# Routed experts in a pipeline of fixed length with a loop of single blocks behind it

## The chip, the cores and the metric

The kernel runs on one core of one Trainium2 chip. The metric is the device time of one execution in microseconds (us). Lines (L2820) are those of the kernel before; in the order listings of the changed kernel they are those of its own file, some 3 to 110 lines further down.

## The reference

Two layers of a decoder trunk on 1024 tokens of 1024 values, in float32. Each layer has a mixer (attention and gated delta rule in layer 0, retention in layer 1) and then a mixture of experts. The change touches only the experts:

```python
g_prob = jax.nn.softmax(xt @ w_group + b_group)            # 4 groups
g_top, g_idx = lax.top_k(g_prob, 1)
e_top, e_idx = lax.top_k(e_logits_of_that_group, 2)        # 8 experts in a group
weights = g_top * softmax(e_top)
expert_id = g_idx * 8 + e_idx                              # 32 experts
# for each of the 2048 (token, expert) pairs:
hid = silu(xs @ w_gate[e]) * (xs @ w_up[e])                # 1024 -> 512
y[token] += (hid @ w_down[e]) * weight                     # 512 -> 1024
```

## The kernel before

**Blocks.** The pairs of an expert are laid out in blocks of `CAP` = 96 rows: `LOW` = 64 low ones and `REST` = 32 more. Every expert has one block, even an empty one; pairs beyond 96 go to overflow blocks behind the 32. Three blocks make a unit, and the number of units is rounded up, so that for up to one overflow block 33 blocks run. `route` works out on the chip, for each place of a block, the tokens (`r.token`), the destinations (`r.dest`), the expert (`r.expert`), a flag that says whether it has more than 64 rows (`r.full`), and in `r.used` the number of units. Its arrays have `NBLK` = 54 columns.

**A block** is, on PE: the gate and up products of the low rows (`gate_up_low`, L2820; two column halves of PE at once), if the flag is set those of the rest rows (`gate_up_rest`, L2830), the transposes of the hidden rows (`hid_turn`, L2840 and L2844), and the down products (`down_low`, L2852, and by the flag `down_rest`, L2860). ACT takes the silu (L2932, L2935), DVE multiplies (L2965), copies the turned hidden rows (L2971) and multiplies with the gate vector (L2977). `turn` (L2813) transposes the gathered token rows for the next block; ACT and DVE bring them to `xT`.

**The pipeline.** `experts` writes the program of each engine by hand. On PE a block b is: gates of b, `hid_turn` of b-1, `turn` for b+1, downs of b-1. So the chain from gates over silu and product to the transposes of one block lies beside the products of its neighbours. Three blocks of unit 0 are written out; then a loop runs over the units, three blocks in its body, as long as `r.used` says. At the head of each unit PE loads the flags of the last block and of its own three (`is_full`, L2889) into registers, and then issues the first low product. Behind the loop stand the `hid_turn` and downs of the last block.

**Weights.** A block's weights are 4 MB for gate and up and 2 MB for down. There are three slots for them (`u` = 0, 1, 2), and the block at place u of a unit takes slot u. The first three loads are issued in `route`'s stage. Then SP goes through a unit in the order gate-up 0, gate-up 1, down 0, gate-up 2, down 1, down 2. A gate-up load waits for the gates of the block that had the slot before, a down load for its downs, and each waits with all that is behind it in the queue.

**Rows.** On POOL the gather of the token rows for the block three places on (L2773) and the scatter of a finished block's rows (L2791) alternate: `gather(m, u)`, `scatter(m - 1, u)`. Each has a small copy of its indices ahead of it.

## Time and profile before

| | us |
|---|---|
| median of 3 runs (lowest, highest) | 3241.58 (3240.41, 3242.32) |
| the profiled execution | 3243.15 |
| its span, first to last instruction | 3241.4 |
| PE busy over the span | 2990.3 (92%) |
| DVE, ACT, POOL busy | 1322.1, 834.3, 701.4 |
| layer 0 experts: first low product to last down product | 965.0 to 1510.1 |
| layer 1 experts: the same | 2613.5 to 3163.6 |
| mean DMA rate over the span | 198 GB/s |

The two expert stages are 1095 us of the span. The page gives averages over all stages: PE is at 92% over all, and the DMA engines at 50 to 60%, while in the expert stages both are close to full. A stage must be read by its own stretches.

### The profile page before, as it was taken

How to read it: one execution, taken by the hardware profiler on the slowest of the kernel's cores; microseconds unless marked ns; L12 is line 12 of the kernel's file. 1: busy time of each engine (PE TensorE's matmuls, PEld its weight loads, DVE VectorE, ACT ScalarE, POOL GpSimd, SP SyncE). 2: the span in 40 equal slices, each digit the busy share in tenths (PEclk: the TensorE clock that was granted, in tenths of full speed). 3: DMA queues.
4: the chain of work that ended last, by engine and by line, in shares of the span. 5: the costliest groups of instructions: out<-in, count | busy, mean ns of one | idle time of the engine just before them, and what ended most of it. 6: DMA issues, size and time to landing. Idle time of an engine off the chain costs nothing. (4 is left out here: it accounts for less than half of the span.)

```text
span 3241.4 us, 45940 instructions
## 1 busy us (share of the span) xinstructions
PE 2990.3 (92%) x16555; PEld 1592.0 (49%) x16556; DVE 1322.1 (41%) x3214; ACT 834.3 (26%) x1707; POOL 701.4 (22%) x1075
## 2 busy tenths in 40 slices
PE   8989999598999999899899999999999989988786
PEld 6446544486444434333466666666444434333333
DVE  4377787573441222122644444444222311222124
ACT  2134343142121111010344445454301111111111
POOL 0000100471111122121633333332100011221213
PEclk9989999799999999999999999999999999999898
DMA  7300055233258999995611011110431297999975
GB/s 298 133 14 1 28 188 176 65 77 107 71 241 350 407 419 412 413 417 231 219 48 38 27 50 51 52 51 14 150 129 44 99 385 309 420 423 407 422 318 224
DMA packets 192256, 642.49 MB, mean 198 GB/s; under 512 B 54964, under 2 KB 114115, under 8 KB 157031
## 3 DMA queue, kind: packets, MB, share of 16 engines
q1 hardware_dynamic: 161670, 589.54, 46.9%
q0 software_dynamic: 20576, 42.01, 3.4%
q10 hardware_dynamic: 9856, 8.92, 0.8%
q8 instruction: 94, 1.54, 0.2%
q14 instruction: 60, 0.48, 0.1%
HBM read 614.61 MB, written 53.79 MB: 206 GB/s over the span
## 5 line engine op out<-in xcount | busy, mean ns | idle before, releaser
L2820 PE MATMUL f1e_pgu<-f1w_gu,f1e_xT 128*64 128x512 f32 x1056 | 251.2, 631 | 66.7 <-DMA f1w_gu<-in_moe_w_up_dram 54.8
L2820 PE MATMUL f0e_pgu<-f0w_gu,f0e_xT 128*64 128x512 f32 x1056 | 245.0, 618 | 30.0 <-issue 14.2
L1926 PE MATMUL mo_py<-mo_w,mo_tiles 128*128 128x512 f32 x512 | 220.9, 592 | 0.0
L2820 PEld LDWEIGHTS f1e_pgu<-f1w_gu,f1e_xT 128*64 128x64 f32 x1056 | 82.4, 145 | 227.6 <-issue 170.7
L2120 PE MATMUL ret_pa<-ret_w,hT_mix 128*128 128x384 f32 x512 | 175.8, 486 | 2.7 <-PEq L3007 2.7
L2820 PEld LDWEIGHTS f0e_pgu<-f0w_gu,f0e_xT 128*64 128x64 f32 x1056 | 80.8, 142 | 183.7 <-issue 169.1
L512 PE MATMUL gc_pq<-hT_mix,gc_w 128*128 128x512 f32 x384 | 169.3, 600 | 0.7 <-PEq L917 0.7
L2971 DVE COPY f1e_hidT<-f1e_ph 128x384 f32<-128x384 f32 x33 | 18.4, 557 | 338.1 <-PE f1e_ph L2844 338.1
L1926 PEld LDWEIGHTS mo_py<-mo_w,mo_tiles 128*128 128x128 f32 x512 | 96.8, 190 | 119.6 <-issue 119.6
L2971 DVE COPY f0e_hidT<-f0e_ph 128x384 f32<-128x384 f32 x33 | 18.4, 557 | 328.3 <-PE f0e_ph L2844 328.3
L2108 POOL TENSOR_TENSOR ret_z<-ret_z,ret_gain 128x256 f32<-128x256 f32 x64 | 46.4, 726 | 454.5 <-DVE ret_z L2409 454.5
L2852 PE MATMUL f1e_pd<-f1w_d,f1e_hidT 128*64 128x512 f32 x528 | 120.6, 598 | 1.0 <-DVE f1e_hidT L2971 1.0
L2852 PE MATMUL f0e_pd<-f0w_d,f0e_hidT 128*64 128x512 f32 x528 | 120.6, 598 | 0.9 <-DVE f0e_hidT L2971 0.9
L2120 PEld LDWEIGHTS ret_pa<-ret_w,hT_mix 128*128 128x128 f32 x512 | 92.6, 190 | 54.9 <-issue 3.0
L2932 ACT ACTIVATE f1e_hs<-f1e_pgu 128x256 f32<-128x256 f32 x33 | 12.6, 383 | 410.1 <-PE f1e_pgu L2820 410.1
L1818 POOL TENSOR_TENSOR mo_z<-mo_z,mo_bias_b 128x1024 f32<-128x1024 f32 x16 | 37.5, 2346 | 370.1 <-DVE mo_z L1795 370.1
L512 PEld LDWEIGHTS gc_pq<-hT_mix,gc_w 128*128 128x128 f32 x384 | 73.1, 192 | 90.4 <-issue 90.4
L1769 DVE TENSOR_TENSOR mo_z<-mo_py,mo_gate_b 128x1024 f32<-128x1024 f32 x16 | 19.6, 1224 | 237.7 <-PE mo_py L1926 237.7
L1926 PE MATMUL mo_py<-mo_w,mixT 128*128 128x512 f32 x256 | 112.8, 600 | 2.5 <-DMA mo_w<-in_hy_w_out_dram 2.5
L2932 ACT ACTIVATE f0e_hs<-f0e_pgu 128x256 f32<-128x256 f32 x33 | 12.6, 383 | 378.3 <-PE f0e_pgu L2820 378.3
L2120 PE MATMUL ret_pb<-ret_wsum,ret_hsum 128*128 128x384 f32 x256 | 91.3, 502 | 2.9 <-issue 2.9
L2787 POOL COPY f1e_didx<-f_dest 128x2 int32 x33 | 5.9, 179 | 380.1 <-DVE f1e_y L2977 304.7
(646 smaller groups left out, 5650.1 us busy)
## 6 DMA issues: line engine op xcount, KB each, us to landing
f0w_gu<-in_moe_w_gate_dram SPq DMA_DIRECT2D x33, 2048.0 KB, 18.6
f0w_gu<-in_moe_w_up_dram SPq DMA_DIRECT2D x33, 2048.0 KB, 26.9
f0w_d<-in_moe_w_down_dram SPq DMA_DIRECT2D x66, 1024.0 KB, 19.7
f1w_gu<-in_moe_w_gate_dram SPq DMA_DIRECT2D x33, 2048.0 KB, 20.0
f1w_gu<-in_moe_w_up_dram SPq DMA_DIRECT2D x33, 2048.0 KB, 31.2
f1w_d<-in_moe_w_down_dram SPq DMA_DIRECT2D x66, 1024.0 KB, 22.3
gc_land<-in_ada_w_dram SPq DMA_DIRECT2D x48, 512.0 KB, 4.9
mixT<-in_ada_w_dram SPq DMA_DIRECT2D x32, 512.0 KB, 4.7
```

What stands on the lines that cost most here:

```text
L512: mm = pe.matmul(pq[u][:, half * 512:(half + 1) * 512], w[u][:, kk, :], g.hT[:, kk, half * 512:(half + 1) * 512], start=(kk == 0), stop=(k ...
L1769: dve.tensor_tensor(z[:, :], y, self.gate_b[:, :], ALU.mult).then_inc(S["zmul"], 1)
L1818: pool.tensor_tensor(z[:, :], z[:, :], self.bias_b[:, :], ALU.add).then_inc(S["done"], 1)
L1926: mm = pe.matmul(py[t % 3][:, half * 512:(half + 1) * 512], rows_of(kk, t), ws[:, kk, half * 512:(half + 1) * 512], start=(kk == 0), stop= ...
L2108: pool.tensor_tensor(zb, zb, gain[:, h, :], ALU.mult).then_inc(S["gained"], 1)
L2120: mm = pe.matmul(bank[:, 0:HW], tokens[:, kk, :], weights[:, kk, :], start=(kk == 0 and not add), stop=(kk == KH - 1), skip_group_check=True)
L2787: pool.tensor_copy(didx[u][:, :], dst).then_inc(slots["didxd"][u], 1)
L2820: mm = pe.matmul(pgu[0][h * LOW:(h + 1) * LOW, :], xT[u][:, kk, 0:LOW], ew.gu[u][:, :, kk, h * FH:(h + 1) * FH], start=(kk == 0), stop=(kk ...
L2852: mm = pe.matmul(pd[0][h * LOW:(h + 1) * LOW, :], hidT_low[:, k % 2, k // 2, :], ew.d[u][:, k, h * DH:(h + 1) * DH], start=(k == 0), stop= ...
L2932: act.activation(hs[0][:, :], pgu[0][:, 0:FH], ACT.Silu).then_inc(S["silu_a"], 1)
L2971: dve.tensor_copy(hidT[:, :], ph[:, 0:4 * CAP]).then_inc(S["hTd"], 1)
```

## The change

Places. `SPARE` = 2 empty places stand ahead of the blocks: block 0 is now at place 2, slot 2 of unit 0, and block 31 at place 33, slot 0 of unit 11. `route` fills the tables two columns further on; they have 57 columns.

The pipeline runs the first `STEADY` = 31 blocks, always: four of them written out (unit 0's last and unit 1), then a loop from unit 2 to unit 10, whose bounds are constants. Behind it stand the `hid_turn` and downs of block 30, and then a loop of single blocks, from place 33 to the last one in use. It has at least one turn (block 31), and one more for each overflow block. All its blocks use slot 0. A weight load in it waits until the block before in slot 0 has done its gates (`gu_free`, counted by ACT) or its downs (`d_free`, by DVE). On PE a turn of the tail's loop is: low gates, rest gates, `hid_turn`, `turn` for the next place, downs; nothing of another block lies between.

The flags are loaded behind the low gate and up product of each block, and not at the head of the unit.

Cut to its core, the diff is:

```diff
+SPARE = 2
+STEADY = NE - 1
+NBLK = SPARE + PAIRS // CAP + NE
+NBLK = -(-NBLK // UNIT) * UNIT
...
     def first_loads(self, sp):
-        for u in range(UNIT):
-            self.load_gu(sp, u, u)
-            self.load_d(sp, u, u)
+        for n in range(UNIT):
+            self.load_gu(sp, (n + SPARE) % UNIT, n)
+            self.load_d(sp, (n + SPARE) % UNIT, n)
...
         @block.sync
-            with sp.Fori(1, units_used(sp)) as m:
+            for m, u in STARTING[UNIT:]:
+                gate_up_weights(m, u, nth(m, u) - 1)
+                down_weights(m, u, nth(m, u) - 1)
+            with sp.Fori(FIRST_UNITS, LAST_UNIT + 1) as m:
                 now = [sp.value_load(expert[0:1, bass.ds(m, 1), u], min_val=0, max_val=NE - 1) for u in range(UNIT)]
                 for u in range(UNIT + 1):
...
+            with sp.Fori(TAIL, places_end(sp)) as p:
+                e = sp.value_load(r.expert[0:1, bass.ds(p, 1)], min_val=0, max_val=NE - 1)
+                sp.wait_ge(S["gu_free"], tail_held(p) - 1)
+                ew.load_gu(sp, 0, e)
+                sp.wait_ge(S["d_free"], tail_held(p) - 1)
+                ew.load_d(sp, 0, e)
...
         @block.gpsimd
-            with pool.Fori(1, units_used(pool)) as m:
+            for m in range(1, 3):
+                for u in range(UNIT):
+                    if m * UNIT + u >= SPARE + UNIT:
+                        gather(m, u)
+                        scatter(m - 1, u)
+            with pool.Fori(3, LAST_UNIT + 1) as m:
                 for u in range(UNIT):
...
+            with pool.Fori(TAIL, places_end(pool)) as p:
+                tail_gather(p + 1)
+                tail_scatter(p)
...
         @block.tensor
+            def block_of(m, u, prior=None, first=False):
+                mb, ub = preceding(m, u)
+                low_gates(u, held(m, u), nth(m, u))
+                if prior is None and not first:
+                    prior = is_full(mb, ub)
+                second = is_full(m, u)
+                rest_gates(u, second)
+                if not first:
+                    hid_turn(nth(mb, ub))
+                turn(*following(m, u))
+                if not first:
+                    downs(ub, held(mb, ub), nth(mb, ub), prior)
+                return second
...
-            with pe.Fori(1, units_used(pe)) as m:
-                prior = is_full(m - 1, UNIT - 1)
-                second = [is_full(m, u) for u in range(UNIT)]
-                for u in range(UNIT):
-                    gates(m, u, second[u])
...
+            with pe.Fori(FIRST_UNITS, LAST_UNIT + 1) as m:
                 for u in range(UNIT):
+                    prior = block_of(m, u, prior if u else None)
+            prior = is_full(*END)
+            hid_turn(nth(*END))
+            downs(END[1], held(*END), nth(*END), prior)
+            with pe.Fori(TAIL, places_end(pe)) as p:
+                low_gates(0, tail_held(p), tail_nth(p))
+                second = pe.value_load(r.full[0:1, bass.ds(p, 1)], min_val=0, max_val=1)
+                rest_gates(0, second)
+                hid_turn(tail_nth(p))
+                turn_rows(0, tail_held(p + 1), tail_nth(p + 1))
+                downs(0, tail_held(p), tail_nth(p), second)
```

ACT and DVE get the same division: four blocks, the loop, the tail's loop. On DVE a turn of the tail is product, copy of the turned rows, `take`, gate multiplication.

**PE, head of the loop over units, layer 0.** The flags (`f_full`) before:

```order
L2902 ISA
L2889 TENSOR_LOAD f_full
L2889 ISA x3
L2889 TENSOR_LOAD f_full
L2889 ISA x3
L2889 TENSOR_LOAD f_full
L2889 ISA x3
L2889 TENSOR_LOAD f_full
L2889 ISA x2
L2877 ISA
L2820 MATMUL f0e_pgu<-f0w_gu,f0e_xT 64x512 x16
```

and now:

```order
L2995 ISA
L2962 ISA
L2754 REGISTER_ALU
L2901 MATMUL f0e_pgu<-f0w_gu,f0e_xT 64x512 x16
L2958 ISA
L2958 TENSOR_LOAD f_full
L2958 ISA x3
L2958 TENSOR_LOAD f_full
L2958 ISA x2
L2969 COMPARE_AND_BRANCH
L2911 MATMUL f0e_pgu<-f0w_gu,f0e_xT 32x256 x32
```

The four loads ahead of the low product (L2820, now L2901) are two behind it, and the other two stand behind the low products of the unit's second and third block.

**PE, the end of layer 0's experts.** The `hid_turn` and downs of the last block before:

```order
L2738 TENSOR_LOAD f_used
L2738 ISA x2
L2836 ISA
L2743 REGISTER_ALU
L2840 MATMUL f0e_ph<-ident,f0e_hid 128x128 x2
L2844 MATMUL f0e_ph<-ident,f0e_hid 64x64 x4
L2889 ISA
L2889 TENSOR_LOAD f_full
L2889 ISA x2
L2866 ISA
L2852 MATMUL f0e_pd<-f0w_d,f0e_hidT 64x512 x8
```

and now, from the downs of block 30 into the tail's loop:

```order
L2933 MATMUL f0e_pd<-f0w_d,f0e_hidT 64x512 x8
L2952 COMPARE_AND_BRANCH
L2941 MATMUL f0e_pd<-f0w_d,f0e_hidT 32x256 x16
L2952 UNCONDITIONAL_BRANCH
L2954 UNCONDITIONAL_BRANCH
L2746 TENSOR_LOAD f_used
L2746 ISA x2
L3001 UNCONDITIONAL_BRANCH
L3001 ISA
L2962 REGISTER_ALU
L2754 REGISTER_ALU
L2901 MATMUL f0e_pgu<-f0w_gu,f0e_xT 64x512 x16
```

Before, the program ends with this block's downs. Now the downs of block 30 stand there with no low product beside them, and the first low product of the tail comes behind the load of the count (`f_used`).

**SP, the first loads of layer 0's expert stage** (the numbers behind `gu` and `d` are the slots). Before, from the first load of the first turn of the loop:

```order
L2689 DMA f0w_gu0<-in_moe_w_gate_dram 128x4096
L2690 DMA f0w_gu0<-in_moe_w_up_dram 128x4096
L2754 REGISTER_ALU
L2689 ISA
L2689 DMA f0w_gu1<-in_moe_w_gate_dram 128x4096
L2690 DMA f0w_gu1<-in_moe_w_up_dram 128x4096
L2694 DMA f0w_d0<-in_moe_w_down_dram 128x2048
L2694 ISA
L2694 DMA f0w_d0<-in_moe_w_down_dram 128x2048
L2689 ISA
L2689 DMA f0w_gu2<-in_moe_w_gate_dram 128x4096
```

and now, from the start of the stage:

```order
L2695 DMA f0w_gu2<-in_moe_w_gate_dram 128x4096
L2696 DMA f0w_gu2<-in_moe_w_up_dram 128x4096
L2700 DMA f0w_d2<-in_moe_w_down_dram 128x2048 x2
L2796 UNCONDITIONAL_BRANCH
L2796 ISA
L2797 TENSOR_LOAD f0_expert
L2797 ISA x3
L2797 TENSOR_LOAD f0_expert
L2797 ISA x3
L2797 TENSOR_LOAD f0_expert
L2797 ISA x2
L2784 REGISTER_ALU
```

The down load of the fourth block (slot 2) now stands ahead of the fifth block's gate-up load; before, it came after it.

## Rows read from the trace of the kernel before

**Rows 1.** Both expert stages: us, five engines busy (x), PEclk, DMA share, GB/s
```profile
972.00:1455.00 483.00, 454.46 (x3366) 193.08 (x3366) 100.02 (x267) 60.03 (x180) 96.90 (x142) 0.98 0.97 403
2624.00:3118.00 494.00, 428.73 (x2824) 177.68 (x2822) 99.44 (x267) 59.16 (x179) 99.23 (x145) 0.94 0.95 393
```

**Rows 2.** PE waits, layer 0 (f0e), layer 1 (f1e): total us, times, longest
```profile
PE f0e_pgu L2820 <- issue: 14.2, 7, 2.9
PE f0e_pgu L2820 <- DMA f0w_gu<-in_moe_w_up_dram: 12.4, 3, 6.5
PE f1e_pgu L2820 <- DMA f1w_gu<-in_moe_w_up_dram: 54.8, 9, 10.7
```

**Rows 3.** Instructions of the gate-up product tile, layer 0: ns min/median/max
```profile
L2830 PE MATMUL f0e_pgu<-f0w_gu,f0e_xT x1088: 378/379/404, 982.2 to 1482.6; 128*32 128x256 f32 x182
```

**Rows 4.** Timeline of PE, layer 0, a block with rests: start us, us
```profile
1011.98 7.09 PE L2820 MATMUL f0e_pgu<-f0w_gu,f0e_xT 128*64 128x512 f32 x32 [2.92 <-issue]
...
1024.47 3.65 PE L2852 MATMUL f0e_pd<-f0w_d,f0e_hidT 128*64 128x512 f32 x16
1028.05 1.93 PE L2860 MATMUL f0e_pd<-f0w_d,f0e_hidT 128*32 128x256 f32 x32
1029.92 7.09 PE L2820 MATMUL f0e_pgu<-f0w_gu,f0e_xT 128*64 128x512 f32 x32
```

**Rows 5.** Timeline of PE: entry into the stage, and the head of a unit
```profile
951.49 11.27 PE L106 MATMUL f0e_pgu<-cos,ident 128*128 128x512 f32 x20 [2.71 <-PEq L2464]
...
1164.66 8.76 PE L2820 MATMUL f0e_pgu<-f0w_gu,f0e_xT 128*64 128x512 f32 x32 [2.50 <-issue]
```

**Rows 6.** PE sequencer, 1160 to 1166 and 1486 to 1500; then its timeline
```profile
L2889 PEldq TENSOR_LOAD <-f_full x4: 287/290/293, 1161.4 to 1163.7; - x4
L2902 PEldq COMPARE_BRANCH  x1: 215/215/215, 1161.0 to 1161.0; - x1
L2883 PEldq COMPARE_BRANCH  x1: 210/210/210, 1492.9 to 1492.9; - x1
1490.26 7.09 PE L2820 MATMUL f0e_pgu<-f0w_gu,f0e_xT 128*64 128x512 f32 x32
```

**Rows 7.** A ten-us stretch of layer 0, columns as in rows 1
```profile
1020.00:1030.00 10.00, 10.00 (x120) 5.00 (x113) 3.01 (x8) 1.67 (x5) 0.00 (x0) 1.00 0.19 77
```

**Rows 8.** PE timeline: gate-up weights of block 30, both layers
```profile
1454.71 8.78 PE L2820 MATMUL f0e_pgu<-f0w_gu,f0e_xT 128*64 128x512 f32 x32 [2.58 <-DMA f0w_gu<-in_moe_w_up_dram]
...
3117.84 10.08 PE L2820 MATMUL f1e_pgu<-f1w_gu,f1e_xT 128*64 128x512 f32 x32 [10.45 <-DMA f1w_gu<-in_moe_w_up_dram]
```

**Rows 9.** Timeline of SP's queue: weight loads issued
```profile
972.31 0.36 SPq L2689 DMA_DIRECT2D f0w_gu<-in_moe_w_gate_dram  x1
...
2624.47 0.35 SPq L2689 DMA_DIRECT2D f1w_gu<-in_moe_w_gate_dram  x1
...
2663.31 23.52 SPq L2694 DMA_DIRECT2D f1w_d<-in_moe_w_down_dram  x4
```

**Rows 10.** Timeline of PE: down products of the last block, both layers
```profile
1506.48 3.65 PE L2852 MATMUL f0e_pd<-f0w_d,f0e_hidT 128*64 128x512 f32 x16 [0.95 <-DVE f0e_hidT L2971]
...
3159.92 3.65 PE L2852 MATMUL f1e_pd<-f1w_d,f1e_hidT 128*64 128x512 f32 x16 [1.05 <-DVE f1e_hidT L2971]
```

**Rows 11.** POOL timeline, layer 0; gather landings from 1478 to 1480, and all
```profile
1473.91 0.18 POOL L2787 COPY f0e_didx<-f_dest 128x2 int32 x1 [15.60 <-DVE f0e_y L2977]
...
1478.30 1.06 POOL L2773 DMA_INDIRECT f_xg<-x,f0e_idx  x1 [0.88 <-POOL f0e_idx L2770]
...
1491.13 0.18 POOL L2787 COPY f0e_didx<-f_dest 128x2 int32 x1 [11.77 <-DVE f0e_y L2977]
...
DMA to landing us min/median/max: 7.0/7.0/7.0
DMA to landing us min/median/max: 7.0/11.7/16.9
```

**Rows 12.** DMA issues from 2624 to 2626: KB each, us to landing
```profile
f1w_gu<-in_moe_w_up_dram SPq DMA_DIRECT2D x1, 2048.0 KB, 13.1
```

More of the change, by code:

```diff
@@ L2743, in reach, with nth, held, tail_nth @@
                 eng.wait_ge(sem, value)
+        def nth(m, u):
+            return m * UNIT + u - (SPARE - 1)
+        def held(m, u):
+            return m + 1 if u >= SPARE else m
+        def tail_nth(p):
+            return p - (SPARE - 1)
+        def tail_held(p):
+            return p - (TAIL - LAST_UNIT - 1)
+        def following(m, u):
+            return (m, u + 1) if u < UNIT - 1 else (m + 1, 0)
+        def preceding(m, u):
+            return (m, u - 1) if u else (m - 1, UNIT - 1)
         expert = r.expert[:, :].rearrange("a (m u) -> a m u", u=UNIT)
@@ L2806, in turn, with turn_rows @@
             def turn(m, u):
-                pe.wait_ge(slots["x_in"][u], m * 16 + 16)
+                turn_rows(u, held(m, u), nth(m, u))
+            def turn_rows(u, landed, n):
+                pe.wait_ge(slots["x_in"][u], landed * 16)
                 for half in range(2):
-                    reach(pe, S["xd" if half else "xa"], m * UNIT + u)
+                    reach(pe, S["xd" if half else "xa"], n - 1)
                     for j in range(4):
@@ L2891, in _ @@
             g.keep_warm(pe, pgu[0][:, :], 10)
-            turn(0, 0)
+            turn(*STARTING[0])
             pe.wait_ge(S["cleared"], 2)
-            second = [is_full(0, u) for u in range(UNIT)]
-            for u in range(UNIT):
-                gates(0, u, second[u])
-                if u:
-                    hid_turn(0, u - 1)
-                turn(*((0, u + 1) if u < UNIT - 1 else (1, 0)))
-                if u:
-                    downs(0, u - 1, second[u - 1])
-            with pe.Fori(1, units_used(pe)) as m:
-                prior = is_full(m - 1, UNIT - 1)
-                second = [is_full(m, u) for u in range(UNIT)]
-                for u in range(UNIT):
-                    gates(m, u, second[u])
-                    hid_turn(*((m, u - 1) if u else (m - 1, UNIT - 1)))
-                    turn(*((m, u + 1) if u < UNIT - 1 else (m + 1, 0)))
-                    if u:
-                        downs(m, u - 1, second[u - 1])
-                    else:
-                        downs(m - 1, UNIT - 1, prior)
@@ L2913, in _ @@
-            end = unit_last(pe)
-            hid_turn(end, UNIT - 1)
-            downs(end, UNIT - 1, is_full(end, UNIT - 1))
+            prior = None
+            for m, u in STARTING:
+                prior = block_of(m, u, prior, (m, u) == STARTING[0])
+            with pe.Fori(FIRST_UNITS, LAST_UNIT + 1) as m:
+                for u in range(UNIT):
+                    prior = block_of(m, u, prior if u else None)
+            prior = is_full(*END)
+            hid_turn(nth(*END))
+            downs(END[1], held(*END), nth(*END), prior)
@@ L2977, in gate_rows, with block_of @@
                     dve.tensor_tensor(y[u][s][:, :], pd[s][:, 0:width], (r.gate if s == 0 else r.gate4)[:, :], ALU.mult)\
                         .then_inc(S[done], 1)
+            def block_of(m, u, first=False):
+                mb, ub = preceding(m, u)
+                n = nth(*following(m, u))
+                if not first:
+                    hid_copy(nth(mb, ub))
+                take(following(m, u)[1], n, n - UNIT)
+                hidden(nth(m, u))
+                if not first:
+                    gate_rows(ub, held(mb, ub), nth(mb, ub))
@@ L2997, in _ @@
-            end = unit_last(dve)
-            hid_copy(end, UNIT - 1)
-            gate_rows(end, UNIT - 1)
+            take(STARTING[0][1], 1, 0)
+            for n, (m, u) in enumerate(STARTING):
+                block_of(m, u, n == 0)
+            with dve.Fori(FIRST_UNITS, LAST_UNIT + 1) as m:
+                for u in range(UNIT):
+                    block_of(m, u)
+            hid_copy(nth(*END))
+            gate_rows(END[1], held(*END), nth(*END))
+            with dve.Fori(TAIL, places_end(dve)) as p:
+                hidden(tail_nth(p))
+                hid_copy(tail_nth(p))
+                take(0, tail_nth(p + 1), tail_nth(p))
+                gate_rows(0, tail_held(p), tail_nth(p))
```

232 lines of the change are left out of this document (127 added, 105 removed).

## The prediction

> **What bounds the kernel now.** The change touches the two expert stages only. So I read, in this order, the table of stretches over both stages, the waits of PE, the PE timeline block by block, the sequencer's own instructions, and the issues and landings of the weights.
>
> The stretches [rows 1] run from the first weight load inside a stage to the last gate-up arrival that PE waited for. PE is busy 454 of 483 us in layer 0 and 429 of 494 in layer 1. The DMA share is 0.97 and 0.95 there, so both resources are nearly full, and the stage goes at the pace of the weights with a little emptiness. PE's waits [rows 2] divide it: layer 0 has 12.4 us for gate-up weights and 14.2 us of "issue"; layer 1 has 54.8 us for weights.
>
> A block with over 64 rows also runs the "rest" products. The rest rows are 64 to a block: 1088/64 = 17 such blocks in layer 0 [rows 3]. Routing the given inputs by the reference gives the same 17, and 10 in layer 1. It also gives the largest expert: 88 pairs in layer 0 (no overflow, so the 33rd block of before is empty) and 100 in layer 1 (one overflow block of 4 rows). In layer 1 the first eight experts are full ones. A block costs PE 7.0 (low) + 1.9 (turns) + 3.6 (down low) = 12.5 us, with 3.6 + 1.9 more for the rests: 17.9 us from one low product to the next after the head of a unit [rows 4].
>
> At the head of a unit PE stands still 2.50 us after a block with rests, and the next low product takes 8.76 instead of 7.09 us, because the granted clock falls to its lower level for a while after the idle time [rows 5, 4]. The sequencer shows why: four flag loads, the first from 1161.4 and the last from 1163.7, some 0.77 us each with their register work, behind a loop branch of 0.215 us [rows 6].
>
> **What the change does, part by part.**
>
> 1. *Flags.* In each block one or two loads now stand behind the low product. The sequencer is ahead there: its branch behind the low product runs at 1492.9, and that product ends at 1490.26 + 7.09 = 1497.35 [rows 6]. Two loads (1.55 us) fit into 4.4 us of lead, so I cost them at nothing. The cover is the queued low product; without it they would cost 0.77 us each. The head of a unit then needs only the branch and register work: 1164.66 less 4 x 0.77 = 1161.6, before the old products end at 1162.16. So PE gains 2.5 + 1.7 = 4.2 us at a head that waits for nothing else. Whether the stage gains it is decided by the weights.
>
> 2. *Weights.* From the first load in the stage (972.3) to the gate-up arrival of block 30 (1454.7) are 482.4 us [rows 8, 9], in which 27 2/3 blocks are moved. I sum what the 49 and 50 ten-us stretches lack to a share of 1.00: 17.7 us in layer 0 (the largest is 8.1, at 1020 [rows 7]) and 29.5 in layer 1. That leaves 16.8 us a block in both: (482.4 - 17.7)/27.67 and (493.4 - 29.5)/27.67. The empty stretches arise where SP waits with the down load of a unit's last slot for a product in the next unit, and the next gate-up load is queued behind it (one such chain of 23.5 us at 2663 [rows 9]). The changed kernel has the same order in SP, one block later. The fourth block's down load now stands ahead of slot 0's, so the queue is empty some 7 us early in layer 0 (984 to 991) and 10 us in layer 1 (2635 to 2645). After that I follow the releases with PE blocks of 12.5 to 17.9 us and no gap at the heads: layer 0 empties for some 1 us more, layer 1 twice for 3.5 (before blocks 6 and 9) and, as before, 4 us later. That makes 8 in place of 17.7, and 21 in place of 29.5: the weights come 9.7 and 8.5 us earlier. The bounds are 0 (the heads' gain is lost in the new order) and 17.7 and 29.5 (no emptiness at all, which the first load chain excludes in part).
>
> 3. *End of layer 0.* 32 blocks, not 33. Gate-up of block 31 arrives at 972.3 + 28.67 x 16.8 + 8 = 1462. Block 28, in slot 0, starts three blocks earlier, at 1411.6. Then PE runs 28, 29, 30 (17.8 with a slow start, 14.4, 16.1) and the drain of 30 without cover: turns 0.9, a copy wait of 0.95 [rows 10], downs 5.5. That ends at 1467.3, later than the weights, so PE decides here. The tail block: 0.5 + 10.7 (gates) + 1.0 (silu and product, nothing beside it) + 0.9 + 1.1 (turns) + 5.5 (downs) = 19.7, so 1487.1 with 0.1 for the loop branch. Before: 1506.48 + 3.65 = 1510.1 [rows 10]. Gain 23.0 us.
>
> 4. *The gather in the tail.* PE's turn for the next place stands ahead of the downs. Its gather is queued in POOL behind the scatter of block 30. As in the loop now, that is 0.9 us from PE's end (1490.3) to the scatter's copy and 4.4 us from such a copy to the gather [rows 11]; I add 1 us for the tail's count, and a landing of 7.0 us in a nearly empty queue: 13.3 us after 1467.3. PE is there after 13.1. I cost it at 0.2 us, inside the rounding; it has no slack, and a landing of 11.7 (median) or 16.9 (longest) would be seen nearly in full.
>
> 5. *End of layer 1.* Still 33 blocks, the last two in the tail. Gate-up of block 31 arrives at 2624.5 + 28.67 x 16.8 + 21, about 3126.5. Gates with a slow clock 8.8: 3135.3. Only then may the load for the overflow block start, since the tail uses one slot: 1.1 us to the up issue, 13.1 us to its landing [rows 12]: 3149.5. Meanwhile PE does the turns and downs of block 31 and stands still for some 7 us. Then 8.8 + 1.35 + 0.97 + 1.1 + 3.65 = 15.9: 3165.4. Before: 3159.92 + 3.65 = 3163.6 [rows 10]. Loss 1.8 us: 8.5 gained on the way, and 10.3 paid for a load that is no longer beside other work.
>
> 6. *The rest.* Routing works on 57 columns instead of 54 and POOL clears two more tiles long before they are needed: 0.1 us. The last scatter of layer 0 now carries real rows: 0.3 us.
>
> The sum: -23.0 + 1.8 + 0.4 = -20.8 us. The profiled execution took 3243.15 us (its span 3241.4), so it would be 3222.3; the median of the runs is 3241.58, 1.6 us lower, and from there **3220.8 us**.
>
> The DMA page of the Trainium skill ("DMA: Bandwidth & Descriptors", Anatomy of one DMA) gives a fit of 2.0 us plus bytes over 436 GB/s. For the 4.19 MB of a gate-up pair that estimate is 11.6 us, 1.9 less than the 13.5 of the row. By it the forecast would be 3218.9. The row is of this kernel with gathers beside it, so it stands.
>
> **The rivals.**
>
> *The emptiness stays* (0.12). SP is still blocked by the last slot's down load, and one block later it may wait for as long. Then both arrivals come 9.7 and 8.5 us later: 3220.8 + 18.2 = 3239.0. For it: the order of the loads in SP is the same. Against: the largest holes follow the heads that now vanish.
>
> *The emptiness goes further* (0.08): another 6 us in each layer, 3209.
>
> *The flags are not covered* (0.05). If a load waited until the products before it were done, 40 of them in a layer at 0.77 us would be 31 us of PE, as much as is saved at the heads. What stays is the missing block, about -8: 3233. Against: at 1161.4 the first load ran while PE was still busy until 1162.16.
>
> *The jumps stall* (0.04). PE's entry into the stage shows 2.71 us of waiting for its sequencer [rows 5]; at five new jumps to a loop's head, its end and the tail that is 13.5 us on the path: 3234. For the loop branch itself the row says 0.215 us. The Trainium skill ("Runtime: NRT & Kernel Launch", Instruction fetch mechanics) says that a taken branch out of the fetched window waits for its target to be fetched; no row shows such a wait at a loop.
>
> *Slower: the tail's gathers are late* (0.08). Three gathers stand in the tails, each behind a scatter and ahead of downs. At 16.9 us instead of 7.0 they cost 9.7 in layer 0, and in layer 1 8.4 and 12, less 3 that the load hides: +27, so 3248. From a landing of about 14.7 us on, the kernel is slower than before. For it: the median is 11.7. Against: most run beside queued weights; this late one took 7.0.
>
> **How the numbers follow.** The forecast has the rest, 0.63. A measurement can tell 0.2%, 6.5 us, from no change. Faster by more than that: the forecast, the further gain, two fifths of the first rival and most of the two small ones, 0.82. Same: 0.10. Slower: 0.08. The range goes from 3204 (beyond the further gain, for sizes of 5 us in each end) to 3238, just short of the first rival's middle; outside lie the slower case, half of the first and a little below: 0.17.
>
> **What would show it.** The heads of units without "issue" waits and with low products of 7.09 us where no weights are late; SP's first two loads 20 us apart; 32 gate-up loads in layer 0; in layer 0 some 25 us from the arrival of block 31's gate-up weights to the last down product; in layer 1 one wait for weights of some 7 us in the last block. It is wrong if the flag loads leave holes between low and rest products, if the tail's turn waits for its gather, or if the ten-us stretches lack as much as before.

## The result and the profile after

The median of the changed kernel is 3220.73 us (4 runs, 3218.24 to 3223.56), beside 3241.2 us for the kernel before (4 runs, 3240.41 to 3242.32). The ratio is 0.9932, 95% interval 0.9919 to 0.9945. The forecast was 3220.8. The profiled execution took 3220.9 us; its span is 3218.6, 22.8 less than before.

A total that fits can hide terms that don't. So I cut both spans at three rows of TensorE: the first low product of a layer's experts, the first product of the combine behind them (f0c, f1c), and the same again in layer 1.

| stretch, us | before | changed | difference | forecast |
|---|---|---|---|---|
| start to layer 0's first low product | 965.0 | 965.9 | +0.9 | +0.1 |
| layer 0's experts, to the combine | 551.3 | 532.4 | -18.9 | -23.0 + 0.3 |
| combine to layer 1's first low product | 1097.2 | 1092.5 | -4.7 | 0 |
| layer 1's experts, to the combine | 556.3 | 556.2 | -0.1 | +1.8 |

The last stretch, from the combine to the end, is 71.6 us in both. Layer 0 gave less than forecast, and a stretch that the change doesn't touch gave 4.7 us. The experiments go after both.

TensorE's waits in the changed kernel (total us, times, longest us), beside [rows 2]:

```profile
PE f0e_pgu L2901 <- DMA f0w_gu<-in_moe_w_up_dram: 26.0, 6, 11.3
PE f1e_pgu L2901 <- DMA f1w_gu<-in_moe_w_up_dram: 59.7, 9, 11.1
```

The 14.2 us of "issue" of layer 0 are gone, and so are the 8.5 us that layer 1 had at four heads. The waits for weights rose from 12.4 to 26.0 us and from 54.8 to 59.7. In layer 0 nearly all that TensorE had stood idle at the heads it now stands idle at the loads, since it meets the weights sooner.

The table of stretches, beside [rows 1] (TensorE's busy time first, the granted clock and the DMA share near the end). Layer 1's line starts at 2618, 16 us behind the stage's first load (2601.62):

```profile
972.00:1462.00 490.00, 462.08 (x3479) 195.66 (x3476) 100.36 (x268) 60.73 (x182) 97.88 (x143) 0.98 0.97 405
2618.00:3105.00 487.00, 431.46 (x2794) 176.17 (x2792) 101.04 (x270) 57.51 (x175) 102.43 (x150) 0.94 0.96 397
```

In ten-us stretches, layer 0 lacks 15.9 us to a full DMA share from 970 to 1450 (17.7 before; forecast 8). Layer 1 lacks 27.7 us from 2600 to 3100, three us before the gates of block 31 (29.5 before; forecast 21). The hole that was 8.1 us deep at 1020 [rows 7] is gone, but there are others, early and late (the last line is layer 1's deepest early one):

```profile
980.00:990.00 10.00, 10.00 (x106) 5.15 (x104) 1.94 (x6) 2.06 (x6) 0.00 (x0) 1.00 0.68 290
990.00:1000.00 10.00, 10.00 (x64) 3.41 (x62) 1.39 (x4) 0.38 (x1) 3.47 (x5) 1.00 0.69 256
1330.00:1340.00 10.00, 10.00 (x72) 3.58 (x70) 2.67 (x8) 0.72 (x3) 2.36 (x4) 1.00 0.75 299
1430.00:1440.00 10.00, 10.00 (x63) 4.24 (x57) 3.33 (x9) 1.67 (x5) 1.59 (x3) 1.00 0.71 282
2610.00:2620.00 10.00, 10.00 (x104) 4.97 (x102) 2.32 (x7) 2.06 (x6) 0.00 (x0) 1.00 0.34 144
```

The end of layer 0 on TensorE's timeline (start us, us, and the idle time before it), beside [rows 8, 10]. It runs from the last products of block 30 through the tail's one block:

```profile
1467.85 3.65 PE L2933 MATMUL f0e_pd<-f0w_d,f0e_hidT 128*64 128x512 f32 x16 [0.88 <-DVE f0e_hidT L3071]
1471.44 1.93 PE L2941 MATMUL f0e_pd<-f0w_d,f0e_hidT 128*32 128x256 f32 x32
1473.55 7.09 PE L2901 MATMUL f0e_pgu<-f0w_gu,f0e_xT 128*64 128x512 f32 x32 [0.18 <-issue]
1480.57 3.66 PE L2911 MATMUL f0e_pgu<-f0w_gu,f0e_xT 128*32 128x256 f32 x64
1485.08 0.48 PE L2921 MATMUL f0e_ph<-ident,f0e_hid 128*128 128x128 f32 x2 [0.86 <-issue]
...
1490.52 1.93 PE L2941 MATMUL f0e_pd<-f0w_d,f0e_hidT 128*32 128x256 f32 x32
```

And the end of layer 1, from the gates of block 31 through the overflow block:

```profile
3103.12 8.78 PE L2901 MATMUL f1e_pgu<-f1w_gu,f1e_xT 128*64 128x512 f32 x32 [3.25 <-DMA f1w_gu<-in_moe_w_up_dram]
...
3125.33 8.56 PE L2901 MATMUL f1e_pgu<-f1w_gu,f1e_xT 128*64 128x512 f32 x32 [5.02 <-DMA f1w_gu<-in_moe_w_up_dram]
3135.23 0.48 PE L2921 MATMUL f1e_ph<-ident,f1e_hid 128*128 128x128 f32 x2 [1.34 <-DVE f1e_hid L3065]
```

### The profile page after: what moved, and what is told of

Its sections match the earlier page's. It is cut to its first block and busy times, and to the rows that moved or that the text cites. A ratio compares the mean times of both kernels' runs of the same rounds, so it can differ in the third digit from the quotient of the medians.

```text
span 3218.6 us, 45601 instructions
## 1 busy us (share of the span) xinstructions
PE 2973.8 (92%) x16489; PEld 1583.7 (49%) x16490; DVE 1317.4 (41%) x3205; ACT 832.2 (26%) x1701; POOL 698.2 (22%) x1074
## 5 line engine op out<-in xcount | busy, mean ns | idle before, releaser
L2901 PE MATMUL f1e_pgu<-f1w_gu,f1e_xT 128*64 128x512 f32 x1056 | 250.7, 630 | 63.0 <-DMA f1w_gu<-in_moe_w_up_dram 59.7
L2901 PE MATMUL f0e_pgu<-f0w_gu,f0e_xT 128*64 128x512 f32 x1024 | 231.5, 605 | 29.5 <-DMA f0w_gu<-in_moe_w_up_dram 26.0
L2901 PEld LDWEIGHTS f1e_pgu<-f1w_gu,f1e_xT 128*64 128x64 f32 x1056 | 81.7, 145 | 223.9 <-issue 221.9
L2901 PEld LDWEIGHTS f0e_pgu<-f0w_gu,f0e_xT 128*64 128x64 f32 x1024 | 75.8, 140 | 174.8 <-issue 173.5
L3071 DVE COPY f1e_hidT<-f1e_ph 128x384 f32<-128x384 f32 x33 | 18.4, 557 | 308.0 <-PE f1e_ph L2925 308.0
L2111 POOL TENSOR_TENSOR ret_z<-ret_z,ret_gain 128x256 f32<-128x256 f32 x64 | 46.4, 725 | 449.9 <-DVE ret_z L2412 449.9
L3024 ACT ACTIVATE f1e_hs<-f1e_pgu 128x256 f32<-128x256 f32 x33 | 12.6, 383 | 413.6 <-PE f1e_pgu L2901 413.6
L2123 PE MATMUL ret_pc<-ret_wsum,ret_hsum 128*128 128x384 f32 x256 | 87.9, 486 | 0.0
## 6 DMA issues: line engine op xcount, KB each, us to landing
f1w_gu<-in_moe_w_gate_dram SPq DMA_DIRECT2D x33, 2048.0 KB, 19.9
```

The costliest lines, as they stand in the source:

```text
L2111: pool.tensor_tensor(zb, zb, gain[:, h, :], ALU.mult).then_inc(S["gained"], 1)
L2123: mm = pe.matmul(bank[:, 0:HW], tokens[:, kk, :], weights[:, kk, :], start=(kk == 0 and not add), stop=(kk == KH - 1), skip_group_check=True)
L2901: mm = pe.matmul(pgu[0][h * LOW:(h + 1) * LOW, :], xT[u][:, kk, 0:LOW], ew.gu[u][:, :, kk, h * FH:(h + 1) * FH], start=(kk == 0), stop=(kk ...
L3024: act.activation(hs[0][:, :], pgu[0][:, 0:FH], ACT.Silu).then_inc(S["silu_a"], 1)
L3071: dve.tensor_copy(hidT[:, :], ph[:, 0:4 * CAP]).then_inc(S["hTd"], 1)
```

## The experiments

Twelve kernels ran. The times are medians, or a single time where the table shows no ratio. The stretches are cut as above, from each kernel's profiled execution.

| run | what | us | ratio to before (95%) | layer 0 | between | layer 1 |
|---|---|---|---|---|---|---|
| before | | 3241.2 | 1 | 551.3 | 1097.2 | 556.3 |
| changed | | 3220.7 | 0.9932 (0.9919 to 0.9945) | 532.4 | 1092.5 | 556.2 |
| e1 | only the flags | 3230.6 | 0.9960 (0.9945 to 0.9974) | 548.0 | 1096.9 | 546.7 |
| e2 | all but the flags | 3236.1 | 0.9985 (0.9970 to 0.9999) | 539.3 | 1092.5 | 566.2 |
| e3 | changed, SP's order | 3203.9 | 0.9881 (0.9864 to 0.9897) | 525.3 | 1092.5 | 548.5 |
| e4 | changed, no overflow block | 3197.7 | 0.9858 (0.9841 to 0.9874) | 532.3 | 1092.6 | 532.3 |
| e6 | changed, no overflow weights | 3213.6 | 0.9901 (0.9884 to 0.9919) | 534.6 | 1090.8 | 550.7 |
| e7 | e3 with another end | 3202.6 | 0.9869 (0.9852 to 0.9887) | 523.6 | 1097.3 | 544.8 |
| e5 | before, 172 dead matmuls | 3243.7 | 0.9999 (0.9989 to 1.0009) | 553.4 | 1091.7 | 556.2 |
| e5b | before, 40 dead matmuls | 3243.6 | 0.9999 (0.9989 to 1.0008) | 554.0 | 1091.6 | 556.1 |
| r1 | before again | 3244.8 | | 554.0 | 1092.2 | 557.0 |
| r2 | changed again | 3220.1 | | 532.3 | 1092.4 | 556.3 |
| e8 | changed, 4 loads of a flag | 3222.3 | | 532.7 | 1091.7 | 556.3 |
| e9 | changed, 8 loads of a flag | 3267.4 | | 561.3 | 1091.5 | 572.8 |

On the chips of the experiments the kernel before had medians of 3243.9, 3243.8, 3244.5 and 3246.4 us; the ratios are to those.

### e1 and e2: the change in two halves

e1 is the kernel before with this edit, and the same for the second place where the flags were read:

```diff
-                second = [is_full(m, u) for u in range(UNIT)]
+                prior = None
                 for u in range(UNIT):
-                    gates(m, u, second[u])
+                    prior, second = gates(m, u, prior)
```

where gates() now reads the flag behind gate_up_low(u).

> The kernel before with only the flags moved: each flag is loaded behind the low product of its block, in the old loop of units, with the 33rd (empty) block of layer 0 and the old end of layer 1. Theory (the flags free the heads of the units, and the weights decide what that is worth): no 'issue' waits at the heads; from the first low product to the combine layer 0 takes some 6 us less than 551.3, layer 1 some 9 us less than 556.3; the kernel 3226, between 3220 and 3232. Rival A (a load behind the low product holds up PE after all, 0.77 us each): 3236 to 3242, with holes between low and rest products. Rival B (the flags bring nothing alone, the fixed pipeline is the gain): 3238 to 3242, with no such holes.

e2 is the changed kernel with the flags at the head again (shown for the loop; the blocks written out ahead of it are changed likewise):

```diff
             with pe.Fori(FIRST_UNITS, LAST_UNIT + 1) as m:
+                prior = is_full(*preceding(m, 0))
+                flags = [is_full(m, u) for u in range(UNIT)]
                 for u in range(UNIT):
-                    prior = block_of(m, u, prior if u else None)
+                    prior = block_of(m, u, prior, False, flags[u])
```

> The changed kernel with the flags of a unit loaded at its head again; fixed pipeline and tail stay. Theory: the heads stand still 2.5 us again; layer 0 keeps only the block that falls away and the shorter end, 8 to 14 us less than before (551.3 from first low product to combine), and layer 1 pays for the load that nothing covers, 5 to 10 us more than before (556.3): the kernel 3232 to 3241. Rival (the fixed pipeline is the gain, the flags are not): 3221 to 3225.

Both theories held. Flags alone: layer 1 lost 9.6 us (forecast 9), layer 0 only 3.3 (forecast 6). The fixed pipeline alone: layer 0 lost 12.0 us, layer 1 gained 9.9. The two halves nearly add up: -15.4 and +0.3 us beside the changed kernel's -18.9 and -0.1. (Layer 0 of the kernel before takes up to 2.7 us more in other executions, see r1 below; against r1's 554.0, e1's gain there is 6.0, as expected.) So in layer 1 the change has two effects of nearly 10 us with opposite signs, and its zero is no sign that nothing happened. e2's last block shows the load that nothing covers at its full price, 7.5 us of idle time:

```profile
3137.00 9.04 PE L2901 MATMUL f1e_pgu<-f1w_gu,f1e_xT 128*64 128x512 f32 x32 [7.50 <-DMA f1w_gu<-in_moe_w_up_dram]
```

### e3: why the weights still have holes

```diff
             for m, u in STARTING[UNIT:]:
                 gate_up_weights(m, u, nth(m, u) - 1)
-                down_weights(m, u, nth(m, u) - 1)
             with sp.Fori(FIRST_UNITS, LAST_UNIT + 1) as m:
+                last = sp.value_load(expert[0:1, bass.ds(m - 1, 1), UNIT - 1], min_val=0, max_val=NE - 1)
                 now = [sp.value_load(expert[0:1, bass.ds(m, 1), u], min_val=0, max_val=NE - 1) for u in range(UNIT)]
-                for u in range(UNIT + 1):
-                    if u < UNIT:
-                        gate_up_weights(m, u, now[u])
-                    if u:
-                        down_weights(m, u - 1, now[u - 1])
+                gate_up_weights(m, 0, now[0])
+                down_weights(m - 1, UNIT - 1, last)
+                for u in range(1, UNIT):
+                    gate_up_weights(m, u, now[u])
+                    down_weights(m, u - 1, now[u - 1])
+            down_weights(*END, nth(*END) - 1)
```

> The changed kernel, with one thing altered in SP's order: the down load of a unit's last slot is queued behind the gate-up load of the next unit's first slot, not ahead of it. Theory (the holes that are left in the DMA queues, 15.9 us in layer 0 and 27.5 in layer 1, arise because SP waits with that down load for a product of the next unit while a free gate-up slot stands behind it): the holes shrink to under 8 us up to the last arrival in each layer, layer 1's last gate-up weights arrive some 10 us earlier, layer 0 gains some 4 us and is then bound by PE; the kernel 3207, between 3203 and 3212. Rival (the holes come from the three slots themselves: SP would wait for the gate-up slot just as long): 3218 to 3224 and holes as before.

The kernel takes 3203.9 us, 1.2% below before, with both stages down (7.2 and 7.7 us below the changed kernel). TensorE waits 15.9 us for gate-up weights in layer 0 and 46.4 in layer 1, beside 26.0 and 59.7. SP's timeline shows why. In the changed kernel a unit's last two down loads stand back to back, and the second waits long:

```profile
1411.90 24.87 SPq L2700 DMA_DIRECT2D f0w_d<-in_moe_w_down_dram  x4
1438.50 0.34 SPq L2695 DMA_DIRECT2D f0w_gu<-in_moe_w_gate_dram  x1
```

An x4 row is two down loads with no gate-up load between them. The kernel before has ten such rows in layer 0 (14 to 28 us long; the one of [rows 9] is layer 1's first), the changed kernel has nine. The gate-up load of the next line was issued 26.6 us after the down load began, and the DMA share fell to 0.71 in the stretch before it. e3 has one x4 row in each layer, where block 30's down load stands ahead of the tail's gate-up load:

```profile
1404.74 18.33 SPq L2700 DMA_DIRECT2D f0w_d<-in_moe_w_down_dram  x4
1424.64 0.35 SPq L2695 DMA_DIRECT2D f0w_gu<-in_moe_w_gate_dram  x1
```

Up to the last arrival ahead of the tail (block 30's, 1440 and 3067 us), e3's ten-us stretches lack 6.7 us in layer 0, under the 8 that were expected, and 10.3 in layer 1, which is over them; 3.9 of these lie in its first 20 us, from 2590 on. Beside the changed kernel's 15.9 and 27.7 us, most of the holes come from the order of SP's queue, not from the three slots.

### e4 and e6: the price of the overflow block

e4 leaves out layer 1's 33rd block (the count of places in use no longer rises with the overflow there, so the four overflow rows are not computed). e6 keeps the block but not its weight loads, so these rows are computed from the weights in slot 0:

```diff
-            with sp.Fori(TAIL, places_end(sp)) as p:
+            with sp.Fori(TAIL, TAIL + 1) as p:
...
-                low_gates(0, tail_held(p), tail_nth(p))
+                low_gates(0, LAST_UNIT + 1, tail_nth(p))
...
-                downs(0, tail_held(p), tail_nth(p), second)
+                downs(0, LAST_UNIT + 1, tail_nth(p), second)
```

> The changed kernel, with the block of overflow rows in layer 1 left out (the four rows of the 33rd block are not computed, layer 1 ends after its 32nd block). It prices the tail's second turn. From the rows of the changed kernel: block 31's gates would be followed by 1 us of silu, the turns and its downs, so the combine starts some 22 us earlier (12.2 us of gates-to-gates with 5.0 us of waiting for weights in it, and 10 of its own end); the kernel 3199. If the second turn were hidden in the weights' time (rival), 3210 or more.

> The changed kernel without the weight loads of the overflow block: it is computed with the weights that lie in slot 0, so its four rows are computed from wrong weights. Everything else of the block stays. Theory: the 5.0 us of idle time before its gates go, and the slow clock behind the idle time (1.7 us) with them: layer 1 takes 549.5 instead of 556.2, the kernel 3214, between 3211 and 3216. Rival A (the turn or the gather of the overflow block ends the wait about as late as the weights): layer 1 555 to 556, the kernel 3220. Rival B (the load also slows other transfers): over 8 us.

e4 took 23.9 us off layer 1 (expected 22): four rows cost 0.7% of the kernel. e6 took off 5.5 us (expected 6.7); the kernel is at 3213.6. The idle time before the overflow block's gates is gone, and with it the lower clock behind it:

```profile
3120.27 3.65 PE L2933 MATMUL f1e_pd<-f1w_d,f1e_hidT 128*64 128x512 f32 x16
3123.76 7.04 PE L2901 MATMUL f1e_pgu<-f1w_gu,f1e_xT 128*64 128x512 f32 x32
```

No turn or gather takes its place; rival A is out. What remains of the 23.9 us, 18.4, is by subtraction the rest of the block's chain; no run divides it further.

### e7: the overflow block in its own slot

e7 is e3 with block 31 moved into the fixed pipeline on all engines, and the loop for overflow blocks on slot 1, under a condition:

```diff
-            down_weights(*END, nth(*END) - 1)
-            with sp.Fori(TAIL, places_end(sp)) as p:
+            gate_up_weights(*LAST, nth(*LAST) - 1)
+            down_weights(*END, nth(*END) - 1)
+            down_weights(*LAST, nth(*LAST) - 1)
...
+            with eng.If(end > TAIL):
+                with eng.Fori(TAIL, end) as p:
...
-                ew.load_gu(sp, 0, e)
+                ew.load_gu(sp, 1, e)
```

> The kernel of run e3 with another end: block 31 (slot 0) stands in the fixed pipeline behind block 30, its gate-up load is queued ahead of block 30's down load, and overflow blocks run in a loop that stands under a condition and uses slot 1 instead of slot 0. So the overflow block's weights in layer 1 can be loaded while blocks 30 and 31 are computed, and the drain of block 30 lies beside the gates of block 31 in both layers. Theory (the price of the changed kernel's end is the load that nothing covers: in e3 6.3 us of idle time before the overflow block's gates and 2.6 us of a slow clock behind it; and block 30's drain without cover, about 1 us of waits, in both layers): layer 1 some 11 us below e3's 548.5, layer 0 some 3 us below 525.3: the kernel 3190, between 3186 and 3195. Rival (the weights' rate sets the end in any case; the overflow block's load then only delays PE elsewhere): layer 1 within 3 us of 548.5, the kernel 3198 to 3203.

This one missed. The experts lost 1.7 and 3.6 us against e3, not 3 and 11, and the median of 3202.6 us can't be told from e3's 3203.9 (their intervals overlap); either is some 17 us below the changed kernel. The rival was right in kind: the overflow block's up load is issued earlier, at 3073.90, but it lands 38.1 us later, beside block 31's loads, where the one that stood alone in the changed kernel took 12.2. The DMA share is 0.84 or more from 3040 to 3100 and 0.46 in the ten us behind. What holds the load up in those last us stays open.

```profile
3091.19 7.09 PE L2920 MATMUL f1e_pgu<-f1w_gu,f1e_xT 128*64 128x512 f32 x32 [0.89 <-DMA f1w_gu<-in_moe_w_up_dram]
3105.45 3.65 PE L2952 MATMUL f1e_pd<-f1w_d,f1e_hidT 128*64 128x512 f32 x16 [0.88 <-DVE f1e_hidT L3097]
3112.45 9.83 PE L2920 MATMUL f1e_pgu<-f1w_gu,f1e_xT 128*64 128x512 f32 x32 [3.35 <-DMA f1w_gu<-in_moe_w_up_dram]
```

The wait before the overflow block's gates fell from e3's 6.32 to 3.35 us and didn't vanish; I had counted the overlap as free. The profiled execution of e7 also has 1097.3 us between the stages, as before has, which leads to the next runs.

### e5, e5b, r1 and r2: the 4.7 us between the stages

The first difference between the traces stands at the start of retention. Kernel before, TensorE's timeline:

```profile
1589.72 2.82 PE L2120 MATMUL ret_pa<-ret_w,hT_mix 128*128 128x384 f32 x8 [2.74 <-PEq L3007]
1592.38 2.74 PE L106 MATMUL ret_pback<-cos,ident 128*128 128x512 f32 x6
1598.04 4.51 PE L2120 MATMUL ret_pb<-ret_wsum,ret_hsum 128*128 128x384 f32 x8 [2.92 <-issue]
```

In the changed kernel ret_pa takes 5.46 us and ret_pb follows without idle time, at 2.82 us. My first theory was where the instructions lie, since retention's stand further back when the experts' code is longer. e5 moves them without altering anything that runs; e5b does the same with 40:

```diff
+            ended = is_full(end, UNIT - 1)
+            downs(end, UNIT - 1, ended)
+            if layer == 0:
+                with pe.If(ended > 0):
+                    g.keep_warm(pe, pgu[0][:, :], 172)
```

> The kernel before with 172 matmuls of TensorE that never run (they stand under a condition that is false, behind layer 0's last down product), so that TensorE's instructions of retention lie as far from the start as in the changed kernel. Nothing that runs is altered. Theory P (the 4.7 us that the changed kernel gains between layer 0's combine and layer 1's first low product hang on where the instructions lie): the 2.92 us of 'issue' idle time before ret_pb goes away, combine to first low product takes 1092 to 1094 instead of 1097.2, and the kernel 3237. Rival Q (they hang on something that the experts leave behind, a queue or a late transfer): 1097.2 as before, the 2.92 us stay, the kernel 3241. In both the expert stages stay at 551.3 and 556.3, but for up to 3 us of waiting at the jump over the matmuls.

> As e5, with 40 matmuls that never run instead of 172. Theory P says that the idle time before ret_pb moves to another instruction or goes; by how much the stage changes it doesn't say, between 1090 and 1100 from combine to first low product, but not the same row with the same 2.92 us. Rival Q: 1097.2 and the same row.

Both gave 1091.7 and 1091.6 us. Theory P named the right numbers, and yet the median of either kernel is that of before. So it had to be asked whether the unchanged kernel does the same by itself:

> The kernel before once more, unchanged, to see what one execution's trace differs from the next. If the stretch from layer 0's combine to layer 1's first low product belongs to the program (rival), it takes 1097.2 us again, with ret_pa at 2.82 us and 2.92 us of idle time before ret_pb. If the chip's clock decides it from one execution to the next (theory), it takes either 1097 or about 1092, and the row of ret_pa says which: 2.82 us goes with 1097, 5.46 with 1092. The two expert stages: 551.3 and 556.3, each within 1 us.

> The changed kernel once more, unchanged. The same question: 1092.5 again with ret_pa at 5.46 us, if it belongs to the program; 1097 with 2.82 us is possible, if the clock decides it from one execution to the next. The expert stages: 532.4 and 556.2, each within 1 us.

It does. r1 is the kernel before, word for word, with 1092.2 us between the stages:

```profile
1596.89 5.46 PE L2120 MATMUL ret_pa<-ret_w,hT_mix 128*128 128x384 f32 x8 [2.74 <-PEq L3007]
1602.15 2.84 PE L106 MATMUL ret_pback<-cos,ident 128*128 128x512 f32 x6
1605.20 2.82 PE L2120 MATMUL ret_pb<-ret_wsum,ret_hsum 128*128 128x384 f32 x8 [0.21 <-issue]
```

So the 4.7 us belong to an execution, not to the program, and theory P falls. (e1 and e7 had the long course too, with 1096.9 and 1097.3 us.) The rows show where the two courses part. ret_pb starts 8.32 us after ret_pa in the first execution (1598.04 less 1589.72) and 8.31 in r1 (1605.20 less 1596.89), so something else lets it go. What differs is TensorE's granted clock. The table of stretches, first for ret_pa and then for ret_pb; the kernel before, first execution:

```profile
1588.00:1593.00 5.00, 3.27 (x10) 2.01 (x11) 3.77 (x4) 1.37 (x2) 2.49 (x2) 1.00 0.60 219
1598.00:1603.00 5.00, 4.96 (x10) 2.85 (x11) 2.79 (x4) 0.01 (x1) 4.91 (x28) 0.66 0.00 0
```

and r1:

```profile
1596.00:1601.00 5.00, 4.11 (x7) 2.30 (x8) 4.22 (x2) 1.28 (x1) 3.32 (x2) 0.50 0.67 275
1605.00:1610.00 5.00, 4.80 (x15) 2.96 (x16) 2.83 (x4) 0.00 (x0) 4.88 (x28) 1.00 0.00 0
```

Both come after the same 2.74 us of idle time. In r1 the clock is at its lower level (1.2 GHz) during ret_pa, where there is room (8.3 us until ret_pb may start), and full again for ret_pb. In the first execution ret_pa runs at full clock (2.4 GHz), is done early, and leaves TensorE idle for 2.92 us; then the low clock falls on ret_pb, which has no room. Why it falls at once in one execution and later in the other stays open.

The clock on ret_pb accounts for 1.7 of the 5.0 us between the two executions (4.51 less 2.82). The next difference is a wait for VectorE; the first execution, then r1:

```profile
1621.42 0.44 PE L2184 MATMUL ret_pturn<-ident,ret_qkr 128*128 128x128 f32 x2 [3.40 <-DVE ret_qkr L2347]
1624.90 0.44 PE L2184 MATMUL ret_pturn<-ident,ret_qkr 128*128 128x128 f32 x2 [1.40 <-DVE ret_qkr L2347]
```

Here TensorE stands 2.0 us longer in the first execution: 3.7 in all so far. One of VectorE's products on the way (L2346) took 3.50 us there and 0.28 in r1. Whether that follows from the clock no run shows, and the rest of the 5.0 us was not placed.

The expert stage of layer 0 moves too: 551.3, 554.0, 553.4 and 554.0 us in four executions of the same live instructions, beside 532.4, 532.3 and 532.7 for the changed kernel (e8 counted in). Compared with the first, the change gave 18.9 us there, compared with r1 21.7.

### e8 and e9: how much the low product covers

```diff
+                for _ in range(3):
+                    is_full(m, u)
                 second = is_full(m, u)
                 rest_gates(u, second)
```

(e9: seven more loads.)

> The changed kernel, with each block's flag loaded four times behind the low product instead of once (the extra values aren't used): 4 or 5 loads of 0.77 us, 3.1 to 3.9 us. Theory (the low product's queue covers 4.4 us of loads): no 'issue' waits before the rest products, both expert stages as in the changed kernel (532.4 and 556.2, within 2 us), the kernel 3220. Rival (a load is only partly covered, or the lead is shorter): an idle time before the rest products of each of some 30 blocks, layer 0 more than 10 us longer.

> As e8, with eight loads of each flag: 8 or 9 loads, 6.2 to 7.0 us. Theory: the cover of 4.4 us ends, and each block waits 1.8 to 2.5 us before its rest products or its turn, 31 times in a layer: some 60 us of TensorE time a layer, of which the weights' slack hides a part; layer 0 30 to 60 us longer, layer 1 10 to 50 us, the kernel 3260 to 3330. Rival (the loads never hold TensorE up, whatever their number): 3220. With e8 it brackets the cover.

Four loads cost nothing: 532.7 and 556.3 us, the kernel's own. Eight cost 28.9 us in layer 0, just under the 30 to 60, and 16.6 in layer 1. The waits of e9 have moved to where the loads are (layer 0 from 970 to 1500 us, then layer 1 from 2600 to 3140):

```profile
PE f0e_ph L2921 <- issue: 24.4, 14, 2.6
PE f0e_pgu L2911 <- issue: 22.1, 16, 2.1
...
PE f1e_ph L2921 <- issue: 34.2, 20, 2.5
PE f1e_pgu L2901 <- DMA f1w_gu<-in_moe_w_up_dram: 15.3, 4, 6.2
```

In layer 1 TensorE stood 59.7 us for weights in the changed kernel; in e9, over the whole stage (to 3194), it stands 19.9 us for them and 48.8 for the flags. Two blocks of e9 with eight loads each show the cover itself. First their rest products on TensorE's timeline, then the loads of the same two blocks on its sequencer (how many, ns, first and last start):

```profile
1007.15 3.66 PE L2911 MATMUL f0e_pgu<-f0w_gu,f0e_xT 128*32 128x256 f32 x64 [1.53 <-issue]
...
1026.05 3.66 PE L2911 MATMUL f0e_pgu<-f0w_gu,f0e_xT 128*32 128x256 f32 x64 [0.88 <-issue]
...
L2958 PEldq TENSOR_LOAD <-f_full x8: 300/310/680, 1001.2 to 1006.4; - x8
L2958 PEldq TENSOR_LOAD <-f_full x8: 300/301/321, 1020.7 to 1025.3; - x8
```

The low products of these blocks end at 1005.63 (998.59 + 7.04) and 1025.16 (1018.07 + 7.09). So the sequencer has a lead of 4.4 and 4.5 us when it comes to the first load, as much as I had read from [rows 6]. From one load to the next it takes 0.66 to 0.74 us here, so by this estimate six fit and eight don't. The waits of e9 run from 0.8 to 2.6 us; the longest stand in the loop's first blocks, which have nine loads.

## Why the prediction was right, and where it wasn't

**Right in the total, for a partly wrong reason.** The median was met within 0.1 us. That the errors cancel is luck. In the first pair of profiled executions four of them leave 2.0 us: layer 0 gave 3.8 us less than forecast and its start came 0.8 us late, layer 1 came out 1.9 us better, and the stretch between the stages gave 4.7 us that were not in the sum. In the second pair (r1, r2) layer 0 has -21.7, layer 1 -0.7 and the stretch between +0.3; there the terms themselves come close, and the rest of the span's -25.2 is the start, 3.8 us earlier, less 0.7 behind the second combine. A sum from one execution each can't be trusted to better than some 5 us here.

**Step 1, flags: right.** No row of the changed kernel shows an "issue" wait at a head, and e8 shows that even four loads are covered. That the weights decide what the heads are worth was right too: e1 took the heads away in both layers and got 3.3 and 9.6 us.

**Step 2, weights: the step that failed, in layer 0.** I let the DMA emptiness fall from 17.7 to 8 us; it is 15.9 up to 1450 alone, and block 31's up load landed at 1466.7 (1438.93 + 27.8), not at 1462. Block 27's gates in the kernel before:

```profile
1404.59 9.95 PE L2820 MATMUL f0e_pgu<-f0w_gu,f0e_xT 128*64 128x512 f32 x32 [3.37 <-DMA f0w_gu<-in_moe_w_up_dram]
```

and block 28's in the changed one:

```profile
1417.85 8.97 PE L2901 MATMUL f0e_pgu<-f0w_gu,f0e_xT 128*64 128x512 f32 x32 [6.13 <-DMA f0w_gu<-in_moe_w_up_dram]
```

That is 439.6 and 451.9 us after the first low product. One block is 16.8 us, so the weights came 439.6 + 16.8 - 451.9 = 4.5 us earlier, not 9.7 (in the second pair 7.1). I followed SP's blocked down load through the first units only and assumed no more holes after them; they come back at 1330 and 1430. e3 shows the cause, which I had under the first rival: the order of SP's loads. In layer 1 block 31's gates started 512.3 us after the first low product, before it was block 30's at 504.3, so they came 504.3 + 16.8 - 512.3 = 8.8 us earlier, forecast 8.5. That fit is luck as well: the emptiness is 27.7 us there, not 21, and with it the 501.5 us from the first load (2601.6) to these gates leave 16.5 us a block over 28.67 blocks, not 16.8. Two terms were off, one against the other; why a block takes less stays open.

**Step 3, end of layer 0: right in kind, 6 us late.** Weights did not set the end, TensorE did, from block 28 on. Block 30's last down product ended at 1473.37, not 1467.3, since block 28 started 6.3 us later than I had it (1417.85, not 1411.6; 0.9 of it is the later start of the stage). From there to the last down product are 19.1 us, forecast 19.7.

**Step 4, the tail's gather: right that it costs nothing, with a misread row.** I allowed 7.0 us for its landing "in a nearly empty queue" and saw no slack. Its row in layer 0:

```profile
f_xg<-x,f0e_idx POOLq DMA_INDIRECT x1, 2.2
```

All its indices are out of range there, since no block follows. But so were those of the row that I took the 7.0 us from: in the kernel before, the gather at 1478.30 is for the place behind the empty 33rd block. The DMA share was 0.58 in the seven us behind its issue, and the gather for the empty 33rd block itself (1457.25) took 11.2 us with the weights' queue full. In the changed kernel the share is 0.12 from 1477 to 1482. So the short landing of 2.2 us goes with the quiet queue, not with the missing rows. The slower rival had its price from gathers beside queued weights; the tail's were all sooner. Layer 1's two landed in 3.8 us (the four overflow rows) and 4.5 us (no rows), and TensorE waited for neither.

**Step 5, end of layer 1: right.** (The terms for block 31's arrival add up to 3127.1, not 3126.5; it changes nothing.) The load that nothing covers was there: 5.0 us of idle time, forecast 7, and e6 priced it at 5.5. It was issued once block 31's gates were done and landed sooner than the 13.1 us of [rows 12]:

```profile
f1w_gu<-in_moe_w_up_dram SPq DMA_DIRECT2D x1, 2048.0 KB, 12.2
```

With the 0.44 us between the two issues (3112.23 and 3112.67 us) the pair took 12.6 us. The fit of the Trainium skill ("DMA: Bandwidth & Descriptors", Anatomy of one DMA), taken for the pair as one transfer, gives an estimate of 11.6 us; the page states it for DMAs that GpSimd issues, and these are SP's. The row from before gave 13.5; this row lies halfway.

**The rivals.** That the emptiness stays was given 0.12. By the sum of the DMA share it was nearly true in both layers (15.9 of 17.7 us, 27.7 of 29.5). In layer 0 it cost little, because TensorE had taken over as the bound by then; in layer 1 the weights came earlier all the same (step 2). Stalls at jumps did not appear: the tail's first gates show 0.18 us of "issue". The Trainium skill ("Runtime: NRT & Kernel Launch", Instruction fetch mechanics) leads one to expect a wait at a jump to code that has not been fetched; at this entry the trace shows none worth the name. Whether the code had been fetched by then, no row says.

## What to carry to other kernels

Where two resources are both nearly full, removing one's stalls can move the time into waits for the other (in e1's layer 0, 14.2 us of "issue" went and 14.2 us of waits for weights came; in layer 1 only 3.3 of 8.5 came back): price the second resource's holes, and look in the issuing queue for what stands behind a blocked load. Here one line moved in SP's order (e3) gave 17 us on top, nearly as much as the whole change. Where a change helps one end of a loop and hurts the other, run the halves apart, for a zero can be +10 and -10. And before a difference in untouched code is explained, profile the unchanged kernel a second time.

## What the runs showed of the hardware

- The same program has two courses from the start of retention on, 1097.2 and 1092.2 us between the same two rows. In the short one the granted clock is at its lower level during ret_pa (5.46 us), in the long one during ret_pb (4.51 us), after the same 2.74 us of idle time; that is 1.7 of the 5.0 us.
- TensorE's sequencer reached the first flag load 4.4 us before a low product of 7.04 us ended, and 4.5 before one of 7.09 (e9). Four loads of a flag cost nothing (e8), eight or nine hold up a block by 0.8 to 2.6 us.
- An indirect gather whose indices are all out of range landed in 2.2 us at a DMA share of 0.12, in 7.0 us at 0.58 and in 11.2 us with the weights' queue full.
